# A third matmul form for experts of up to 32 tokens, and gate and up weights loaded as one contiguous run per partition

## The reference, cut to what matters

```
for e in range(MOE_EXPERTS):                       # 16 experts, 1024 -> 512 -> 1024
    he = jax.nn.silu(h @ w_gate[e]) * (h @ w_up[e])
    out = out + combine[..., e:e + 1].astype(h.dtype) * (he @ w_down[e])
```

## Time and profile before

| | |
|---|---|
| runs of the kernel before | 2169.95 us median of 3 (2161.38 to 2170.52) |
| profiled execution | 2167.39 us, of it 2165.0 us in the span of the trace |
| PE matmul busy | 1907.9 us, 88% of the span |
| DVE, ACT busy | 574.1 us (27%), 381.7 us (18%) |
| moved by DMA | 620.85 MB, mean 287 GB/s |
| first expert stage | from 373.98 to about 645 us of the span |

### The profile page before, as it was taken

One profiled execution on the slowest core, in us unless ns is written; L12 is line 12 of the kernel. 1 busy time (PEld: TensorE's weight loads), 2 busy tenths in 40 slices (PEclk: granted clock), 3 DMA queues, 4 the chain that ended last, 5 costly groups with the idle time before them and its releaser, 6 DMA issues.

```text
span 2165.0 us, 27897 instructions
## 1 busy us (share of the span) xinstructions
PE 1907.9 (88%) x10445; PEld 1020.2 (47%) x10446; DVE 574.1 (27%) x1118; ACT 381.7 (18%) x693; POOL 9.2 (0%) x25
## 2 busy tenths in 40 slices
PE   8978978999998998999978789889999777889886
PEld 6665534666654875554443233334433332334333
DVE  3443342222224122342342111212221221122213
ACT  1022201122222003341111111111111110111111
POOL 1000000000000000000000000000000000000000
PEclk9978999999999998999989999999999998999999
DMA  8941352999995454221359998889999999999990
GB/s 271 380 170 40 117 187 86 353 375 371 375 368 181 138 176 174 78 70 47 155 195 414 414 416 321 356 344 366 403 415 412 416 415 415 413 405 415 415 382 24
DMA packets 175507, 620.85 MB, mean 287 GB/s; under 512 B 12253, under 2 KB 21148, under 8 KB 142536
## 3 DMA queue, kind: packets, MB, share of 16 engines
q1 hardware_dynamic: 175096, 616.96, 73.4%
q10 hardware_dynamic: 208, 0.67, 0.1%
HBM read 616.56 MB, written 1.05 MB: 285 GB/s over the span
## 4 chain that ended last, share of the span: by engine, by line
PE 75%; DMA 14%; issue 4%; DVE 4%; ACT 2%; SPq 0%; ACTq 0%; DVEq 0%
DMA ring<-exp_w 14%; PE pairs L1736 13%; PE pairs L2091 12%; PE pairs L1727 7%; PE pairs L2012 5%; PE pairs L2191 4%; PE pairs L2220 4%; PE pairs L2248 4%; PE pairs L2211 3%; PE pairs L1779 3%; PE pairs L1940 3%; PE pairs L2041 3%; PE pairs L2177 2%; PE pairs L2094 2%; PE pairs L1822 2%
## 5 line engine op out<-in xcount | busy, mean ns | idle before, releaser
L2091 PE MATMUL pairs<-ring,r_at 128*32 128x512 f32 (+1 forms) x2176 | 354.0, 651 | 77.1 <-DMA ring<-exp_w 39.8
L2091 PEld LDWEIGHTS pairs<-ring,r_at 128*32 128x32 f32 (+1 forms) x2176 | 88.3, 123 | 232.8 <-issue 220.8
L1736 PE MATMUL pairs<-ring,x_T 128*128 128x512 f32 (+1 forms) x480 | 184.9, 542 | 3.3 <-ACT x_T L870 1.5
L1727 PE MATMUL pairs<-x_T,ring 128*128 128x256 f32 x656 | 146.6, 386 | 7.0 <-DVEq L996 4.0
L2191 PE MATMUL pairs<-ring,r_big 128*32 128x512 f32 (+1 forms) x896 | 123.8, 595 | 32.3 <-issue 32.3
L1727 PEld LDWEIGHTS pairs<-x_T,ring 128*128 128x128 f32 x656 | 126.1, 193 | 26.1 <-DVEq L996 6.2
L2248 PE MATMUL pairs<-r_at,r_big 128*128 128x512 f32 x256 | 127.6, 644 | 9.1 <-issue 9.1
L1395 DVE TENSOR_SCALAR r_big<-r_u,rank 128x128 f32 x66 | 15.9, 284 | 448.0 <-PE pairs L2059 423.4
L2220 PEld LDWEIGHTS pairs<-r_big,r_mix 128*128 128x128 f32 x1056 | 124.5, 194 | 18.4 <-issue 18.4
L1736 PEld LDWEIGHTS pairs<-ring,x_T 128*128 128x128 f32 x480 | 85.2, 194 | 96.6 <-issue 94.3
L2220 PE MATMUL pairs<-r_big,r_mix 128*128 128x128 f32 x1056 | 124.8, 277 | 2.6 <-DVE r_big L1395 2.6
(11 more groups left out here) (384 smaller groups left out, 1922.3 us busy)
## 6 DMA issues: line engine op xcount, KB each, us to landing
ring<-exp_w SPq DMA_DIRECT2D x192, 2048.0 KB, 20.6
ring<-w_in SPq DMA_DIRECT2D x23, 2048.0 KB, 9.2
ring<-w_gate SPq DMA_DIRECT2D x16, 2048.0 KB, 11.6
ring<-w_up SPq DMA_DIRECT2D x16, 2048.0 KB, 13.7
ring<-w_down SPq DMA_DIRECT2D x16, 2048.0 KB, 9.7
ring<-mod_w SPq DMA_DIRECT2D x12, 2048.0 KB, 16.9
ring<-w_out SPq DMA_DIRECT2D x4, 2048.0 KB, 7.8
ring<-w_branch SPq DMA_DIRECT2D x3, 2048.0 KB, 11.2
```

The source lines that it names most:

```text
L1727: ins = mm(out[:, ct], w[:, k, c0 + P * ct:c0 + P * ct + P], xT[:, k], start=(k == 0), stop=(k == nk - 1))
L1736: ins = mm(out[:, t, 0:n], xT[:, k, P * t:P * t + P], w[:, k, c0:c0 + n], start=(k == 0), stop=(k == nk - 1 and bias is None))
L2091: mm(out, stat(k), w_[:, k % 2, 512 * q:512 * q + 512], start=(k == 0), stop=False)
```

## The change

Class 0 is now "up to 32 tokens", class 1 "up to 64", class 2 "up to 128", class 3 more (`ranks` has one operation more on DVE). Class 0 has bodies of its own on every engine. Gate and up are computed by one function, `gate_and_up`, which waits for both slots; in class 0 four matmuls of 256 columns stand side by side, two for up and two for gate, all in `ps[0]`, and `PD` rises by 2 at the end. The down product of class 0 also has four side by side, as two partial sums for each half of the columns, which the scatter adds because the pick repeats its 32 slots four times (`slot_table`). Classes 2 and 3, which had straight code, are two-round loops.

SP loads row `8*p + t` into partition `p` for gate and up, one piece of 16 KB per partition. To match, the first block's normalised rows are turned through a strided view (`XN1_by_rows`), and the router weights and the norm's gain are loaded in the same order. The turned picks move from `ps[1]` to `ps[0]`, columns 512 to 767, and PE waits before them until ACT has copied the next expert's gathered rows. DVE reads the class before its waits, and picks its slots by it.

```diff
-            for c, w in enumerate((H2, P, T)):
-                with eng.If(size == c):
-                    body(w)
...
-                src = w[bass.ds(e * (nk * P), nk * P), :].rearrange("(t p) n -> p t n", p=P)
+                rows = w[bass.ds(e * (nk * P), nk * P), :]
+                src = rows.rearrange("(t p) n -> p t n" if kind == 2 else "(p t) n -> p t n", p=P)
...
-                    link(v.tensor_scalar(some, cum[0:1, 0], float(P // 2), None, ALU.is_gt))
+                    link(v.tensor_scalar(some, cum[0:1, 0], float(P // 4), None, ALU.is_gt))
+                    link(v.scalar_tensor_tensor(out=some, in0=cum[0:1, 0], scalar=float(P // 2), in1=some,
+                                                op0=ALU.is_gt, op1=ALU.add))
...
-                slots = iota if b == 1 else slots_of[:, bass.ds(size_of(dve, e) * P, P)]
+                slots = slot_table[b][:, bass.ds((size_of(dve, e, 3 if b == 1 else 4) if size is None else size) * P, P)]
...
-                    ins = nc.tensor.transpose(o[:, P * k:P * k + P], src[:, t, P * k:P * k + P], ident)
+                    cols = src[:, t, k] if r == 1 else src[:, t, P * k:P * k + P]
+                    ins = nc.tensor.transpose(o[:, P * k:P * k + P], cols, ident)
...
+            def gate_and_up(j, load_values, e, size):
+
+                pe.wait_ge(slot_loaded[j % RING], load_values[0])
+                pe.wait_ge(slot_loaded[(j + 1) % RING], load_values[1])
+                w_gu = [slot1(j + n, KD) for n in range(2)]
...
+                with pe.If(size == 0):
+                    for k in range(KD):
+                        for q in range(4):
+                            ins = mm(ps[0][H4 * q:H4 * q + H4, 0:256], XG[:, k, 0:H4],
+                                     w_gu[1 - q // 2][:, k, 256 * (q % 2):256 * (q % 2) + 256], start=(k == 0),
+                                     stop=(k == KD - 1))
+                    ins.then_inc(PD, 2)
+                with pe.If(size == 1):
+                    for i in range(2):
+                        for k in range(KD):
+                            for h in range(2):
+                                ins = mm(ps[i][H2 * h:H2 * h + H2, 0:256], XG[:, k, 0:H2],
+                                         w_gu[i][:, k, 256 * h:256 * h + 256], start=(k == 0), stop=(k == KD - 1))
+                        ins.then_inc(PD, 1)
...
-                    for f in range(4):
+                    for f in (0, 2, 1, 3) if w == H4 else range(4):
...
+                            if w == H4:
+
+                                at, to = H2 * (f % 2) + H4 * (f // 2), H2 * h + H4 * (f // 2)
+                                ins = mm(ps[2][to:to + H4, 0:512], HTF[:, at:at + H4], cols, start=(f % 2 == 0),
+                                         stop=(f % 2 == 1))
...
-                half_up(j, value_of(j, i, 3), ps[0], size)
+                gate_and_up(j, [value_of(j + n, i, 3) for n in range(2)], e, size)
                 pe.wait_ge(sem("pickT_ready1"), e + 1)
-                half_up(j + 1, value_of(j + 1, i, 3), ps[1], size)
                 scatter1(e, size_before)
...
                 half_down(j + 2, value_of(j + 2, i, 3), size)
-                turn_picks1(buf, size)
+                pe.wait_ge(sem("xg_ready1"), e + 2)
+                turn_picks(1, buf)
```

More of the change, by code:

```diff
@@ L1257, in _, with slots_of_sizes @@
                     mod_scale(24, 24)
+            def slots_of_sizes(table, widths):
+                for c, w in enumerate(widths):
+                    link(v.tensor_copy(table[:, P * c:P * c + P].rearrange("p (q s) -> p q s", s=w),
+                                       iota[:, 0:w].unsqueeze(1).broadcast_to([P, P // w, w])))
             def routing_ahead(n, before_all):
@@ L1985, in ranks @@
                 mm(o[:, n:2 * n], tri[:, 1, P:T], sel[:, 1, 0:n], start=True, stop=True).then_inc(PD, 1)
-            out_and_logits(1, "wo", [slot(I[f"wo{h}"], KD) for h in range(2)], AT1, XN1,
+            out_and_logits(1, "wo", [slot(I[f"wo{h}"], KD) for h in range(2)], AT1, XN1_by_rows,
                            [r_wr1[:, 20 * k:20 * k + 32] for k in range(KD)], 20)
@@ L1990, in _, with slot1 @@
             all_free("rk1")
[L1996 to L2009, removed]
-                    for k in range(KD):
[L2011 to L2015, removed]
+            def slot1(j, nk):
+                return ring[:, (j % RING) * SLOT:(j % RING + 1) * SLOT].rearrange("p (t n) -> p t n", t=nk)
@@ L2037, in body, with columns_in_turn @@
                             cols = w_[:, f, 512 * h:512 * h + 512]
-                            if w == H2:
+                            if w == H4:
+                                at, to = H2 * (f % 2) + H4 * (f // 2), H2 * h + H4 * (f // 2)
+                                ins = mm(ps[2][to:to + H4, 0:512], HTF[:, at:at + H4], cols, start=(f % 2 == 0),
+                                         stop=(f % 2 == 1))
+                            else:
                                 at = P * (f % 2) + H2 * (f // 2)
                                 ins = mm(ps[2][H2 * h:H2 * h + H2, 0:512], HTF[:, at:at + H2], cols, start=beg, stop=end)
[L2042 to L2045, removed]
                     ins.then_inc(PD, 1)
-                by_size(pe, size, body)
+                def columns_in_turn(nt):
+                    at = (j % RING) * SLOT
+                    with nc.Fori(0, 2, engines=[pe.engine]) as h:
+                        for f in range(4):
+                            for t in range(nt):
+                                mm(pairs[:, bass.ds(h * 512 + 2048 + 1024 * t, 512)],
+                                   HTF[:, 512 * t + P * f:512 * t + P * f + P], ring[:, bass.ds(h * 512 + at + D * f, 512)],
+                                   start=(f == 0), stop=(f == 3))
+                with pe.If(size == 0):
+                    body(H4)
+                with pe.If(size == 1):
+                    body(H2)
+                with pe.If(size == 2):
+                    columns_in_turn(1)
+                    mark(ps[3][0:1, 0:1]).then_inc(PD, 1)
+                with pe.If(size == 3):
+                    columns_in_turn(2)
+                    pe.drain().then_inc(PD, 1)
             def up_parts(w):
```

141 lines of the change are left out of this document (87 added, 54 removed).

## The result

Over 12 runs of each, the changed kernel takes 2175.1 us (2171.76 to 2188.05) and the kernel before 2165.7 (2161.38 to 2170.52). The ratio is 1.0047 [1.0031, 1.0062]: a little slower, where 2142 was forecast. The profiled execution took 2173.01 us, 2170.4 of it in the span.

The account below looks back on a forecast made before the run. PE bounds the first expert stage, with transfers close behind; faster 32-wide experts, then limited by loads at 415 GB/s, end it at 617.5 instead of 645.0, so 2167.4 less 27.5 is 2139.9, forecast as a 2142 us median, range 2134 to 2156.

Parts of the forecast that it names:

- PE sets the pace: First expert stage before the change: PE's gapless 16.82 us per expert is the bound, with transfers nearly equal.
- The loops of classes 2 and 3 aren't executed: Small steps of the first expert stage: these bodies don't run, and no time was counted for them.
- PE runs 4 to 7 from the ring's stock, 443.2 + 4 x 11.8: First stage: experts 4 to 7 use weights already loaded, 11.8 us each, ending at 490.4; then PE waits for loads.
- The gain doesn't arrive: Rival: narrow class not taken, or the next part's load waits give the gain back; 2160 to 2171 us, chance 0.08.
- The narrow products are bound by issue: Rival: 32-wide gate and up stay at 6.91 us, expert 15.0 us, gain 16.2 us, 2153 us; chance 0.08.
- Piece length doesn't matter: Rival: first-stage loads stay at 387 GB/s, 16.26 us per expert, gain 18.1 us, 2152 us; chance 0.10.
- PE stays at the lower clock: Rival: idle time holds PE at 1.2 GHz, 32-wide experts take 23.6 us, 61 us added, 2231 us; chance 0.04.
- the own case: The prediction's main case for the whole kernel: 2137 (loads at 430 GB/s, 31 us gained) to 2148 us, chance 0.70.
- The start of the stage: First expert stage: reading the class before the first pick, plus one small operation, starts PE's experts 1.0 us later.
- The hiding of silu, the multiply and the copy ahead of the picks: 32-wide experts: the 1.92 us scatter covers silu and multiply (0.384, 0.424 us); the 1.85 us down product covers ACT's copy.
- A load-bound expert at 15.16 us: First stage once loads set the pace: three loads of 5.05 us each at 415 GB/s make 15.16 us per expert.
- The cold start at 2.3 us: After waits for loads, PE's first groups run slower, 2.3 us in all, counted ahead of 64-wide expert 12.

Follow-up runs that it names:

- short_code: Changed kernel without PE's bodies for classes 2 and 3 in the first expert stage, which no expert takes; 2146.23 us, ratio 0.9893.
- dead_code: Kernel before with 64 matmuls more per expert (some 16 KB of program) in a branch never taken; 2227.97 us, one run.
- short_pieces: short_code with gate and up loaded in 2 KB pieces again and the row order of before; 2154.79 us, ratio 0.9933.
- dead_half: Kernel before with 32 matmuls more per expert (some 8 KB of program) in a branch never taken; 2193.76 us, ratio 1.0124.
- never32: Changed kernel with the first threshold at -1, so that every expert runs the 64-wide form; 2183.19 us, ratio 1.008.
- quarter_loads: Changed kernel loading only the first quarter of each expert weight's bytes in stage one; 2145.03 us, one run.
- contig_only: Kernel before with only the contiguous loads of gate and up and the row order belonging to them; 2164.61 us, ratio 1.0004.

## Why the prediction was wrong

**What bounds the kernel.** "PE sets the pace" held, and so did the transfers as the next bound: short_code meets them at 414 GB/s. But a third bound lay between the two, and I had no term for it.

**The step that failed** is in two sentences. "The loops of classes 2 and 3 aren't executed" gave them a price of nothing, and "PE runs 4 to 7 from the ring's stock, 443.2 + 4 x 11.8" took PE's program to be there whenever PE wants it. Bodies that are not executed are brought nevertheless (17 pieces against 7 when they are left out), and beside the loads the kernels that waited got one piece in 6.0 to 6.7 us on average. An expert of the changed kernel brings some 2.6 pieces (37 from 380 to 620 us, over 14 experts), and its own 11.6 us ask for one in 4.5; it got one in 6.3. (That 2.6 x 6.3 is the 16.5 us of experts 4 to 11 proves nothing, as both come from the same stretch; what proves it are short_code, dead_code and the landings at the ends of the waits.) A 64-wide expert of 16.8 us just hides this; a 32-wide one of 11.6 can't. Experts 4 to 7, forecast 11.8 us apart, took 17.3, 16.3, 15.9 and 20.1 us. The gain went there, about 5 us for each, in waits inside the experts, and the forecast's 415 GB/s was never asked for. It could have been seen: the page of before has a row for the queue that brings programs (190 pieces, 3.11 MB), and the order rows shown ahead of the prediction list the bodies that no expert executes. Dividing the pieces in a stage by its experts gives 2.4 for each before (34 in 240 us), one in 7.1 us; asking for one in 4.9 us (11.8 us for 2.4) was the thing to doubt.

**The rivals.** "The gain doesn't arrive" comes nearest by its time (2160 to 2171, with 2175.1 measured), but its two reasons weren't the ones. "The narrow products are bound by issue" falls: gate and up took 3.59 to 3.77 us. "Piece length doesn't matter" could not show in the changed kernel, and short_pieces speaks against it. "PE stays at the lower clock" was partly right in kind: expert 12 started cold (8.81 for 7.06), and dead_half shows such starts after waits of 2.2 to 2.5 us, but the granted clock of the stage was 0.92 and not 0.5. One slip in the sums: loads at 430 GB/s and 31 us gained give 2139 and not 2137 for the lower end of the own case.

**What was right.** Each piece of PE: gate and up 3.59 to 3.77 (3.70), down 1.85 (1.85), picks 0.37 (0.37); the two transposes of the hidden rows take 0.11 to 0.20 and not 0.37, and the gather up to 3.86 and not 3.59. Together 11.6 for 11.80. The start of the stage was 1.2 us later by the change, where 1.0 was forecast: the first pick follows the ranks by 369.05 - 367.78 = 1.27 us where it was 0.23, and with 0.20 for the new operation that is 1.24. The chain of the changed kernel there:

```profile
367.58 0.20 DVE rank L1373
...
369.05 0.29 DVE r_big L1413
```

The hiding of silu, the multiply and the copy ahead of the picks held wherever the program was there: short_code's experts 4 and 5 follow one another in 11.61 us with no wait inside. A load-bound expert at 15.16 us: 15.4 in short_code. The cold start at 2.3 us was 1.75. And the whole: short_code, which is the changed kernel nearly without this one bound, took 2146 where 2142 was forecast, inside the range of 2134 to 2156. It gained 20 us on the median of the kernel before beside it (2166.68), where 28 were forecast.

The Trainium skill, page "Runtime: NRT & Kernel Launch", section "Instruction fetch mechanics", says that an engine's instructions are fetched ahead in sequence, in blocks of 16 KiB, by the sequencer's own queue, and that crossing a block costs little, mostly hidden. The trace agrees on the size (3.16 MB in 193 pieces) and on the sequence: skipped bodies are brought. On the cost it agrees for the kernel before and not for the changed one, where the waits sum to over 30 us in this stage.

**What stays open.** A piece is moved in about 1 us, yet pieces came 5 to 6 us apart on average where PE waited for them. What starts the next piece, and why it starts later beside the loads, no run shows; nor whether a wait comes from the jump over a skipped body or from the amount of code alone. Single pieces stood 3.1 us apart, so the averages are no fixed rate, and they can't forecast the size of a loss: dead_half and never32 both missed.

## What to carry to other kernels

Where an engine's program is written out and a faster form is added beside the old ones, count the bytes of all forms for each step, executed or not, against the time that the step will take: here one 16 KB piece in 7 us of PE's own time cost at most 0.9 us of waiting at a time, one in 5.8 us or less made PE wait for over 2 us again and again, and the price of a form that is never taken can be greater than the gain of the one that is. Before forecasting a shorter step, read the pieces of the instruction queue in that stretch as one more bound beside engine and loads. An "issue" wait in the middle of straight code is its sign, with a piece landing 1.3 to 1.9 us before the engine goes on; leaving out bodies that these inputs never use is the quickest proof.

## What the runs showed of the hardware

- Where PE waited for its program, pieces of 16 KB came one in 6.0 to 6.7 us on average over 120 us with loads at 310 to 413 GB/s, and one in 5.2 us at 121 GB/s (quarter_loads). Single ones stood 3.1 us apart (changed kernel, 390 to 394 us).
- A piece was moved in about 1 us, and PE went on 1.3 to 1.9 us after it had landed, in all nine waits of over 2 us of the changed kernel.
- 16 KB of program per expert that is never executed cost 3.8 us per expert (dead_code, one run), 8 KB 1.9 (dead_half, 30.5 us over 16).
- Four of five waits of PE of 2.2 to 2.5 us were followed by a group of 64 records in 8.81 us instead of 6.91, the granted clock of such a group being 0.81 against 1.00 (dead_half).
- Loads in pieces of 16 and 4 KB moved 414 GB/s, in 2 and 4 KB 391, with the DMA engines busy all the time (shares of 1.00 and 1.04; short_code, short_pieces). In a kernel that doesn't ask for more, the long pieces lowered the DMA engines' busy share from 1.01 to 0.92 at 370 GB/s (before, contig_only).
